# Two-block model on one core: conditioning panels gathered as rows of one PSUM bank and turned into columns four times, with five chains of waits put in another order

## The reference, cut to what matters

```python
def second_block(x, c, positions, w_ada, b_ada, ...):
    c_act = jax.nn.silu(c)
    for l in range(DEPTH_2):
        h = hybrid_layer(h, c_act, cos, sin, w_ada[l], b_ada[l], ...)

def hybrid_layer(x, c_act, cos, sin, w_ada, b_ada, w_in, ...):
    ada = c_act @ w_ada + b_ada
    shift, scale, gate = jnp.split(ada, 3, axis=-1)
    u = x * (1.0 + scale[:, None, :]) + shift[:, None, :]
    proj = jnp.einsum("bsd,dp->bsp", u, w_in)
    ...
    return layer_norm(DEEPNORM_ALPHA * x + gate[:, None, :] * out, ln_g, ln_b)

def s5_branch(u, ...):
    ...
    y = y * jax.nn.sigmoid(y @ w_glu + b_glu)

merged = g_ssm * (y_ssm @ w_up_ssm) + g_attn * (y_attn @ w_up_attn)
h = h + merged @ w_out
```

## Time and profile before

| | before |
|---|---|
| median of 3 runs | 1056.01 us (1053.74 to 1057.05) |
| the profiled execution | 1058.53 us, of which the span is 1056.7 us |
| TensorE busy | 1011.7 us, 96% |
| DVE, ACT, GpSimd busy | 696.7, 545.7, 375.9 us (66%, 52%, 36%) |
| mean granted TensorE clock | 0.984 of full |
| read from HBM | 177.26 MB |

### The profile page before, as it was taken

How to read it: one execution, slowest core, us unless ns; L and a number is a source line. 1 busy time by engine, 2 the same in 40 slices (tenths; PEclk the granted TensorE clock), 3 DMA queues, 4 the chain that set the end, 5 groups by cost and what they waited for, 6 DMA issues and landing times.

```text
span 1056.7 us, 19594 instructions
## 1 busy us (share of the span) xinstructions
PE 1011.7 (96%) x8132; PEld 957.7 (91%) x8132; DVE 696.7 (66%) x1052; ACT 545.7 (52%) x631; POOL 375.9 (36%) x159
## 2 busy tenths in 40 slices
PE   7998999989999999999999999999899999999996
PEld 6986887878999999989999999999699999999995
DVE  4959889786432222366878995865559789868563
ACT  5455565655544434457554745543466547446532
POOL 3079683003688887510066430000100566300000
PEclk8998999999999999999999999999899999999998
DMA  8652555766765665464744546553557354564601
GB/s 271 209 160 81 160 160 160 239 201 222 249 192 174 194 183 185 157 186 144 229 140 142 177 149 194 168 191 120 154 165 239 120 160 148 172 200 144 205 12 40
DMA packets 159496, 179.58 MB, mean 170 GB/s; under 512 B 5040, under 2 KB 141744, under 8 KB 159408
## 3 DMA queue, kind: packets, MB, share of 16 engines
q1 hardware_dynamic: 159024, 177.22, 53.3%
q0 software_dynamic: 384, 1.10, 0.3%
HBM read 177.26 MB, written 1.05 MB: 169 GB/s over the span
## 4 chain that ended last, share of the span: by engine, by line
PE 75%; DVE 11%; issue 7%; ACT 5%; DMA 1%; POOL 1%; SPq 0%; DVEq 0%; ACTq 0%; POOLq 0%
PE pg L1803 65%; DVE p_bu L1681 2%; PE p_s L1886 2%; DVE area L1246 2%; PE p_y L1957 1%; ACT w_hi L928 1%; ACT u_hi L903 1%; PE pg L1824 1%; PE p_s L1779 1%; DVE area L1264 1%; DVE rows L1288 1%; DVE area L1250 1%; PE p_s L1940 1%; DMA area<-in_c_state 1%; PE p_bu L1940 1%
## 5 line engine op out<-in xcount | busy, mean ns | idle before, releaser
L818 POOL TENSOR_TENSOR w_lo<-raw,w_hi 128x2048 fp32r<-128x2048 f32 x61 | 284.6, 4675 | 304.1 <-ACT w_hi L928 304.1
L928 ACT ACTIVATE w_hi<-raw 128x2048 fp32r<-128x2048 f32 (+3 forms) x153 | 275.1, 1804 | 68.3 <-PE pg L1803 30.7
L1803 PE MATMUL pg<-u_hi,w_hi 128*128 128x256 f32 x1536 | 213.7, 291 | 15.5 <-ACT u_hi L903 11.3
L1237 DVE TENSOR_TENSOR w_lo<-raw,w_hi 128x2048 fp32r<-128x2048 f32 (+2 forms) x92 | 190.5, 2083 | 54.6 <-ACT w_hi L928 54.4
L1803 PEld LDWEIGHTS pg<-u_hi,w_hi 128*128 128x128 f32 x1536 | 196.2, 194 | 26.0 <-issue 9.8
L1803 PE MATMUL pg<-u_lo,w_hi 128*128 128x256 f32 x1536 | 202.6, 285 | 0.0
L1803 PE MATMUL pg<-u_hi,w_lo 128*128 128x256 f32 x1536 | 200.2, 283 | 0.0
L1803 PEld LDWEIGHTS pg<-u_lo,w_hi 128*128 128x128 f32 x1536 | 193.9, 194 | 0.0
L1803 PEld LDWEIGHTS pg<-u_hi,w_lo 128*128 128x128 f32 x1536 | 191.4, 192 | 0.0
L934 ACT ACTIVATE area<-pg 128x512 f32<-128x512 f32 (+1 forms) x92 | 54.1, 588 | 155.2 <-PE pg L1803 143.3
L1681 DVE SCALAR_TENSOR_TENSOR p_bu<-area,par,p_bu 128x256 f32<-128x256 f32 x232 | 93.9, 483 | 0.9
(11 more groups left out here) (217 smaller groups left out, 1354.6 us busy)
## 6 DMA issues: line engine op xcount, KB each, us to landing
raw<-in_w_in SPq DMA_DIRECT2D x68, 1024.0 KB, 5.3
raw<-in_w_ff SPq DMA_DIRECT2D x32, 1024.0 KB, 5.6
raw<-in_w_ada SPq DMA_DIRECT2D x24, 1024.0 KB, 5.3
raw<-in_w_gate SPq DMA_DIRECT2D x8, 1024.0 KB, 7.8
raw<-in_w_o SPq DMA_DIRECT2D x8, 1024.0 KB, 5.2
raw<-in_w_out SPq DMA_DIRECT2D x4, 1024.0 KB, 7.0
raw<-in_w_b_out SPq DMA_DIRECT2D x4, 1024.0 KB, 5.0
raw<-in_w_c_out SPq DMA_DIRECT2D x4, 1024.0 KB, 5.2
```

Source lines behind the costliest of these rows:

```text
L818: pool.tensor_tensor(w_lo[:, s, 0:n], raw[:, r, 0:n], w_hi[:, s, 0:n].bitcast(F32), ALU.subtract).then_inc(sem(f"raw_free{r}"), 1)
L928: act.activation(dst, src, ACT.Copy).then_inc(*(c.event("w_hi", q["s"]) if i == len(parts) - 1 else c.step()))
L1237: ins = dve.tensor_tensor(dst, src, hi.bitcast(F32), ALU.subtract)
L1803: ins = pe.matmul(pg[g % 2][0:m, i * T:i * T + T], w[:, k, a:a + m], x[:, k, :], start=x is x_hi and w is wh and (i, k) == turns[0], stop= ...
```

## The change

1. *Rows in one bank.* Panel i's stationary operand is now a 32-column strip that is zero except for one column, which holds silu_c and stands at the panel's place in its group (`selector`). So each panel adds its own row to one accumulation: panels 0 to 8 in a pg bank, 9 to 16, 17 to 19 and 20 to 23 in p_z. A group is copied once (`ada_rows`, ACT) and turned once (`ada_columns`, two matmuls with a `pick` of 32 columns, into p_c). The strips lie in the tiles mask2 and odd_z, so the causal mask is filled later, and the second strip is written by GpSimd after the last head (`ada_selector`).
2. *Start.* Pieces 2 and 3 of x are loaded from ACT's queue; SP waits for pieces 0 and 1 only; the load of params waits for piece 0. DVE makes all rows first, then u_lo, then w_lo.
3. *Heads.* Six filler matmuls before `stick_fails(1)`; ACT preloads its table for the first two heads.
4. *Behind glu.* Ada panels 11, 12 and 13 stand together; the load of the first up_ssm panel is pulled in front of 12's.
5. *Layers.* GpSimd makes two of the eight u_hi tiles, and halves are made ahead of `ada_rows(3)`; the two latent roots are split, with halves between them; `gate_take` of the last gate goes in front of a conv part.

```diff
-ADA_PARTS = ((0, 14), (14, 17), (17, 20), (20, 24))
+ADA_PARTS = ((0, 9), (9, 17), (17, 20), (20, 24))
+STRIP = 32
+MIDDLE = 11
...
+        if m == 1:
+            step("keep_clock", 6, 1)
         step("stick_fails", m)
-        step("ada_turn", m)
...
         ada_panel(m + 1)
-        step("ada_take", m + 1)
...
+            step("ada_selector")
+            step("ada_rows", 0)
             ada_panel(9)
-            step("ada_turn", 8)
-            step("ada_take", 9)
             ada_panel(10)
-            step("ada_turn", 9)
-            step("ada_take", 10)
...
-    step("ada_turn", 10)
+    step("ada_columns", 0)
     step("s5_out", HEADS - 1)
...
     half("glu", 0, "w_glu", W)
     ada_panel(11)
-    step("ada_take", 11)
+    load("up_ssm", 0, 0)
+    ada_panel(12)
+    ada_panel(13)
     step("glu_mul")
     step("split", "yg")
-    ada_panel(12)
-    step("ada_turn", 11)
-    step("ada_take", 12)
     for n in range(2):
         panel("up_ssm", 0, n, "w_up_ssm", 0, 512 * n, WT, 512, 2)
...
-        if n < 2:
-            step("ada_turn", 12 + n)
-        if n == 0:
-            ada_panel(13)
-            step("ada_take", 13)
...
-        step("latent_roots", l)
+        step("latent_root", l, 0)
+        step("high_ahead", count["split"] + 3)
+        step("latent_root", l, 1)
+        step("table_set", "sigmoid_and_others")
...
+            if h == HEADS + 1:
+                step("gate_take", len(panels) - 1)
...
-        step("gate_take", len(panels) - 1)
...
-            for j in range(4):
+            for j in range(2):
                 sp.dma_start(h[:, 2 * j:2 * j + 2, :], t["x_t"].rearrange("(k p) n -> p k n", p=P)[:, 2 * j:2 * j + 2, :]
                              ).then_inc(sem(f"x_landed{j}"), 16)
-            for j in range(4):
+            for j in range(2):
                 sp.wait_ge(sem(f"x_landed{j}"), 16)
...
+            for j in range(2, 4):
+                act.dma_start(h[:, 2 * j:2 * j + 2, :], t["x_t"].rearrange("(k p) n -> p k n", p=P)[:, 2 * j:2 * j + 2, :]
+                              ).then_inc(sem(f"x_landed{j}"), 16)
...
+            def ada_selector(_, __):
+
+                pool.wait_ge(sem("logw"), over("logw", HEADS - 1))
+                pool.wait_ge(sem("silu_c"), over("silu_c"))
+                pool.memset(odd_z[:, :], 0.0).then_inc(*k.step())
+                pool.wait_ge(*k.last)
+                pool.tensor_copy(selector[1][:, :, MIDDLE], silu_c[:, :]).then_inc(*k.event("selector_late"))
...
                     for k in range(KT):
-                        strip = slice(32 * (k % 4), 32 * (k % 4) + 32)
-                        ins = pe.matmul(pg[g % 2][strip, 0:256], silu_c[:, k:k + 1].broadcast_to([P, 32]), w[:, k, :], start=k < 4, stop=k >= KT - 4)
-                    ins.then_inc(sem("groups"), 1)
+                        strip = slice(STRIP * (k % 4), STRIP * (k % 4) + STRIP)
+                        ins = pe.matmul(rows[strip, 0:256], selector[part > 0][:, k, MIDDLE - row:MIDDLE - row + STRIP], w[:, k, :],
+                                        start=row == 0 and k < 4, stop=i == end - 1 and k >= KT - 4)
```

More of the change, by code:

```diff
@@ L144, in norm_steps @@
         step("norm", k)
[L145 to L151, removed]
+        for n in range(3):
+            ada_panel(i + n)
         step("modulate", key[1])
-        step("ada_take", i + 2)
+        step("ada_rows", part_of(i))
     step("table_set", "sqrt_and_others")
@@ L631, in build @@
         mer = kf
+        selector = [a[:, 0:KT * (STRIP + MIDDLE)].rearrange("p (k w) -> p k w", k=KT) for a in (mask2, odd_z)]
         pg = [bank("pg0"), bank("pg1")]
@@ L701, in operand_of, with high_piece @@
             return own.get(q["job"], "u"), q["layer"]
+        def high_piece(key, j):
+            if key in (("u", 0), ("u", 1)) and j == 3:
+                return sem("u_high"), over("u_high", key[1])
+            return sem("hi"), over("hi", key, j)
         def sums_before(key):
@@ L878, in modulate @@
                 pool.wait_ge(sem("scale1"), over("scale1", l))
-                for j in range(2):
+                pool.wait_ge(sem("groups"), OPERANDS["u", l]["after"] + 1)
+                for j, dst, name in ((0, tmp, "u_rows"), (3, u_hi, "u_high")):
                     pool.wait_ge(sem("ln_rows"), over("ln_rows", l - 1, j))
                     for i in (2 * j, 2 * j + 1):
-                        pool.tensor_scalar(tmp[:, i, :], h[:, i, :], scale1[:, i:i + 1], shift1[:, i:i + 1], ALU.mult,
-                                           ALU.add).then_inc(*(k.event("u_rows", l, j) if i % 2 else k.step()))
+                        pool.tensor_scalar(dst[:, i, :], h[:, i, :], scale1[:, i:i + 1], shift1[:, i:i + 1], ALU.mult,
+                                           ALU.add).then_inc(*(k.event(name, l) if i % 2 else k.step()))
             def rope_k(l, _):
@@ L888, in rope_k @@
                 pool.tensor_copy(kf[NOPE:P, :, :], spread(kpe[NOPE:P, :], 2 * ROPE, HEADS, T)).then_inc(*k.event("k_spread", l))
-            steps = dict(panel=panel, gate_ahead=panel, s5_diag=s5_diag, table=table, modulate=modulate, rope_k=rope_k)
+            def ada_selector(_, __):
[4 more added lines that the diff above has]
+                pool.tensor_copy(selector[1][:, :, MIDDLE], silu_c[:, :]).then_inc(*k.event("selector_late"))
+                pool.wait_ge(sem("groups"), find("ada", 0, 8)["g"] + 1)
+                pool.memset(mask2[:, :], 0.0).then_inc(*k.step())
+                for lo in (0, 256):
+                    pool.wait_ge(*k.last)
+                    pool.affine_select(out=mask2[:, lo:lo + P], in_=mask2[:, lo:lo + P], compare_op=ALU.is_ge,
+                                       fill=-BIG, base=0, pattern=[[-1, P]], channel_multiplier=1).then_inc(*(k.event("mask2") if lo else k.step()))
+            steps = dict(panel=panel, gate_ahead=panel, ada_selector=ada_selector, s5_diag=s5_diag, table=table, modulate=modulate, rope_k=rope_k)
             for kind, a, b in ORDER:
@@ L1009, in norm, with ada_rows @@
                 square_root(("norm", k), 0, D, RMS_EPS)
-            def ada_take(i, _):
-                if i:
-                    act.wait_ge(sem("ada_turned"), over("ada_turned", i - 1))
-                g = find("ada", i // 12, i % 12)["g"]
-                take(g, root[:, 1, :], pg[g % 2][:, 0:256])
+            def ada_rows(part, _):
+                if part:
+                    act.wait_ge(sem("ada_turned"), over("ada_turned", part - 1))
+                i = ADA_PARTS[part][1] - 1
+                q = find("ada", i // 12, i % 12)
+                if q["groups"]:
+                    take(q["g"], root[:, 1, :], pg[q["g"] % 2][:, 0:256])
+                else:
+                    act.wait_ge(*slot_free(q))
+                    fn(root[:, 1, :], p_z[:, 0:256], ACT.Copy).then_inc(*c.event("ada_rows", part))
             def panel(p, _):
@@ L1300, in norm @@
                         ins.then_inc(*(c.event("rows", "u0", j // 2) if j % 2 else c.step()))
-                        if j == 3:
-                            low_halves(first_splits(1, ahead))
-                        if j % 2 and j >= 3:
-                            low("u0", j // 2 - 1)
-                    low("u0", 3)
+                    for j in range(4):
+                        low("u0", j)
+                    low_halves(first_splits(1, ahead))
                 elif k == 2:
@@ L2060, in _ @@
             pe.wait_ge(sem("const"), over("const", "ones"))
-            steps = dict(norm_sums=norm_sums, keep_clock=keep_clock, panel=panel, ada_turn=ada_turn, s5_turn=s5_turn, bu=bu, s5_out=s5_out,
+            steps = dict(norm_sums=norm_sums, keep_clock=keep_clock, panel=panel, ada_columns=ada_columns, s5_turn=s5_turn, bu=bu, s5_out=s5_out,
                          stick_scores=stick_scores, stick_fails=stick_fails, stick_out=stick_out,
```

143 lines of the change are left out of this document (77 added, 66 removed).

## The result

| | before | changed |
|---|---|---|
| median of the compared runs | 1054.34 us (9 runs, 1051.77 to 1058.19) | 1058.75 us (9 runs, 1057.65 to 1060.94) |
| ratio, 95% interval | | 1.0041 (1.0027 to 1.0055) |
| the profiled execution | 1058.53 us, span 1056.7 | 1058.74 us, span 1057.0 |
| mean granted TensorE clock | 0.984 | 0.985 |

The account below looks back on a forecast made before the run. TensorE, busy 96% of the span, was taken as the bound, with 45 us of waits. Terms -4.6 - 3.3 + 13.6 - 0.85 - 1.7 - 1.3 - 1.7 - 3.1 = -3.0 on 1058.5, less 2.5 to the median, gave 1053.0 us; range 1043 to 1061.

Parts of the forecast that it names:

- Start, -4.6: Program start: earlier first weight panel and DVE making all rows first win 4.6 us, bounds -1.0 and -5.8.
- -3.7 for the earlier panel: Start: SP waits for two x pieces only, so the first weight panel is issued about 3.7 us sooner.
- -0.9 for DVE's order: Start: all rows before any w_lo removes PE's 1.71 us wait at 20.09, half of it won at half clock.
- 8.42 us later PE starts: Start: PE begins 8.42 us after the first panel's issue, as from 8.10 to 16.52 us in the profile.
- Heads, -3.3: Head loop: turns taken out and a row wait gone, less a new selector wait, win 3.3 us; bounds 0 and -5.0.
- DVE waits for PE only 2.0 + 1.8 us in this loop: Head loop: of 3.4 us of removed turns, only gains up to 3.8 us count before DVE sets the pace.
- Stall behind glu, +9.5: Behind glu: up_ssm's second panel loads only after ada 11, its halves precede glu's product; up_ssm starts 9.5 us later.
- The half clock behind it, +3.3 (net +4.1): From up_ssm to norm_sums(1,0): PE's idle of about 10 us brings the half clock, costing 3.3 us of a possible 0 to 5.2.
- forecast -0.8 and +1.6: Behind up_ssm: a 0.76 us wait at 224.33 goes; an extra DVE w_lo, less a turn, delays norm_sums by 1.6 us.
- The slower rival: norm_sums(1,0) and up_ssm: two long low-clock stretches, 5.2 us each, make +4.1, 1060.1 us; chance 0.22.
- Later, -8.65: ff1 and layers: -0.85 turns, -1.7 layer entries, -1.3 w_hi wait, -1.7 latent roots, -3.1 last gate's eviction.
- moving the last gate's eviction ahead of a conv part removes two of 1.6: Layers: evicting the last gate before a conv part removes two PE waits of 1.6 us, -3.1.

Follow-up runs that it names:

- e7: The kernel before with the start's edits alone: 1050.54 us, 0.9969 of before.
- second execution: The kernel before, unedited, profiled once more: 1054.63 us, span 1052.8.
- e2: The changed kernel with the last gate's `gate_take` put back behind the conv part: 1057.74 us, 1.0026 of before.
- e3: The changed kernel with DVE's w_lo of the first merge panel moved between the two conv parts: 1056.24 us, 1.0021 of before.
- e11: The kernel before with only the early eviction of the last gate: 1056.43 us, 1.0027 of before.
- e14: The changed kernel with both up_ssm loads before ada 11, DVE's first merge w_lo and va_lo between conv parts, `modulate_columns(0)` behind `ada_end(0)`: 1042.24 us, 0.9883 of before.
- e13: The kernel before with the start's edits, early gate eviction, and DVE's first merge w_lo and va_lo between the conv parts: 1048.02 us, 0.9944 of before.

## Why the prediction was wrong, step by step

- **Start, -4.6: the sum right, by luck.** Measured -4.2 in the trace and -3.7 alone (e7), and PE's third pass came at 20.53 us, forecast 20.5. But the parts were -3.7 for the earlier panel and -0.9 for DVE's order, and it was the other way round. The panel was issued at 5.97 us, not 4.4, and PE's first matmul came 1.0 us sooner (14.91 against 15.94; 0.2 in e7). The passes behind it gave 3.2 (5.62 us from the first to the third, against 8.82). The step "8.42 us later PE starts" did not hold (8.94 in the changed kernel, 9.85 in e7), and the waits that DVE's order removes were priced at half of one of them.
- **Heads, -3.3: wrong, +0.4 measured.** The step that failed is "DVE waits for PE only 2.0 + 1.8 us in this loop; beyond 3.8 us DVE sets the pace". Those 3.8 us came from the execution that had its low clock at 95 us. In the second execution DVE waits in the heads for this alone:

```profile
DVE area L1246 <- DVE odd_z L1246: 0.5, 1, 0.5
```

  and the busy times there (length; PE, PEld, DVE, ACT, POOL; clock) are

```profile
110.00:185.50 75.50, 74.32 (x620) 57.79 (x618) 68.75 (x112) 47.53 (x69) 45.18 (x28) 1.00 0.49 159
```

  DVE works 68.75 of 75.50 us and never waits for PE, so the turns taken from PE win less than their 3.4 us. Two places of the same work, before and changed:

```profile
101.03 1.13 PE L1940 MATMUL p_bu<-area 32*128 32x256 f32 x4
97.57 1.12 PE L1974 MATMUL p_bu<-area 32*128 32x256 f32 x4
...
178.65 0.41 PE L1824 MATMUL pg<-raw,silu_c 128*32 128x256 f32 x2
173.71 0.41 PE L1857 MATMUL pg<-raw,mask 128*32 128x256 f32 x2
```

  The lead of the changed kernel grows there from 3.5 to 4.9 us, by 1.5. The rest of the step lies around it: of the start's 4.2 us 0.8 are lost before 97.57, and 1.1 are lost behind 173.71. At that end the new wait for the selector came as named, 1.9 us, and the last S5 output waits 1.3 us for DVE (fifth and sixth rows above). Against the first execution, from which the term was worked out, the same step measures -4.2 (up_attn began at 192.29 us there), so the turns and waits had been read off an execution that is not like the second. It could have been suspected: that execution was 2.5 us above the median, and half of 10.40 us at half clock is 5.2. I took the 2.5 off as a constant and did not ask where they lay.
- **Stall behind glu, +9.5: right, +9.9 measured.** The chain came as the rows said; the load was issued at 204.14 us and its w_hi began 5.20 us later, against the 5.27 us from the earlier trace rows. The changed kernel:

```profile
204.14 0.37 SPq L743 DMA_DIRECT2D raw<-in_w_up_ssm  x1
...
209.34 1.91 ACT L939 ACTIVATE w_hi<-raw 128x2048 fp32r<-128x2048 f32 x1 [5.18 <-DMA raw<-in_w_up_ssm]
211.28 2.29 DVE L1251 TENSOR_TENSOR w_lo<-raw,w_hi 128x2048 fp32r<-128x2048 f32 x1 [11.29 <-ACT w_hi L939]
213.49 1.22 DVE L1260 TENSOR_TENSOR area<-area 128x1024 f32<-128x1024 f32 x1
214.79 1.06 ACT L914 ACTIVATE va_hi<-area 128x1024 fp32r<-128x1024 f32 x1 [3.54 <-DVE area L1260]
```

- **The half clock behind it, +3.3 (net +4.1): mis-sized.** From up_ssm to norm_sums(1,0) the loss grew by 1.4 us. The wait of 2.6 us at norm_sums came as forecast, but over half of the low stretch lay inside the long wait, where it costs nothing, and not behind it:

```profile
210.10:215.99 5.89, 0.00 (x0) 0.50 1.10 349
215.99:220.80 4.81, 4.81 (x24) 0.55 1.06 335
220.80:245.40 24.60, 20.91 (x170) 1.00 0.39 125
```

  The 4.81 us at 1.2 GHz cost 1.7 us: PE's next matmuls at the full clock, at 220.84, are 7.7 us later than in before's second execution (213.15), where up_ssm's first were 6.0. The terms beside it (forecast -0.8 and +1.6) came to -0.3 together. The slower rival (two long stretches, 1060.1 us) had the sign, but its mechanism did not occur: the clock is full behind the first stretch and at the second wait (1.00 from 245 to 250 us too).
- **Later, -8.65: wrong, -3.3 measured.** The small terms hold up: with ff1's turns, layer 0's entry and latent roots and its gate, 4.0 us of the forecast, the offset falls by 4.6, from 7.4 to 2.8 us at 608.61. The step that failed is "moving the last gate's eviction ahead of a conv part removes two of 1.6". It did remove the waits, and I did not ask what the earlier PE would trigger. It triggers GpSimd's w_lo, which then holds DVE: +2.7 us by the ln_a sums (637.29 less 631.84, against +2.8 at the gate), and the wait of 2.06 us at layer 1's ln_a sums is the same again. e2, e3 and e11 to e14 show this: the part forecast at -3.1 costs 1.0 us in the change (e2; not clear of the noise) and 1.6 in the kernel before (e11), or 2.8 by e11's ratio.

In the trace the sum missed by 7.2 us (+4.2 against -3.0): heads 3.7, later 5.4, start and stall 0.8, less 2.7 for the stretch behind the stall. The change fails by one stall of 10 us that one load's place in the list makes; with that and DVE's order mended, the same ideas are worth 12.0 us (e14), of which 5.8 beyond the start, the gate and the conv order alone (e13).

## What to carry to other kernels

When an engine is made to run ahead, ask which instruction it releases on the other engines, and whether that one now begins in front of something it must not precede: here 1.7 us won by PE cost DVE 4.4 us per layer, because GpSimd was released first, and DVE's critical instructions had to be put ahead of it. Take a second execution of the kernel before before resting a term on its waits: a stretch at half clock makes waits on other engines that another execution of the same kernel does not have. And a load's place in a ring of slots is worth working out from rows, event by event: that term (9.5 us, 9.9 measured) was the largest of the sum, and its chain came row by row as worked out.

## What the runs showed that I had not expected

- Two DVE instructions on 128x8 took 3.92 and 4.42 us beside GpSimd's w_lo (0.17 us each when alone), a w_lo 6.72 for 2.29, a va_lo 4.17 for 1.22. The SCALAR_TENSOR_TENSOR of the conv, which takes one operand from PSUM, ran through GpSimd's w_lo of 619.92 us without a loss: 16 in 6.48 us in the changed kernel, against 6.50 at 607.04, where GpSimd did nothing.
- The same kernel before ran 10.40 us at the low clock after a wait of 2.25 us in one execution, and in the other 7.00 us of it 10 us earlier, after a wait of 1.11 us; a wait of nearly the same length there (1.10 us, ending at 85.71) cost the first execution no clock. In the wait of 10.2 us the clock fell while PE stood, at about 210.1 us, so only 4.81 us of work lay behind it before the clock was back. How long PE had stood was no measure here of how much work then ran at the low clock.
